# Scan of an RWKV-7 layer: kappa products and query masks moved from a tile's head to its last two levels, prefix sums parted over two levels

## The chip, the core and the metric

The kernel runs on one core of a Trainium2 chip. Time is the device time of one execution in microseconds (us). The engines are TensorE (PE in the profile; its weight loads are PEld), VectorE (DVE), ScalarE (ACT), GpSimd (POOL) and SyncE (SP), which here only issues DMAs. Each runs its own instruction queue in order, and they meet at semaphores.

## What is computed

A two-layer encoder trunk on an input of 256 positions by 1024 channels, all in float32. Both layers have a half-step SwiGLU feed-forward network ahead of and behind their mixer. The mixer of layer 0 is a Hyena convolution beside windowed attention. That of layer 1 is RWKV-7 time mixing in both directions, and the change is in there. Its reference, cut to what matters:

```python
def step(S, inp):
    r_t, w_t, k_t, v_t, a_t, b_t = inp
    sa = jnp.einsum('zbhvk,zbhk->zbhv', S, a_t)
    S = S * w_t[..., None, :] + sa[..., :, None] * b_t[..., None, :] + v_t[..., :, None] * k_t[..., None, :]
    return S, jnp.einsum('zbhvk,zbhk->zbhv', S, r_t)

xs = (shared(r), time_major(decay), time_major(k_dir), shared(v), shared(-kk), time_major(b_dir))
_, ys = lax.scan(step, jnp.zeros((2, B, H, N, N), f32), xs)
y = ys[0] + ys[1][:, ::-1]            # then a norm per head, a bonus, a gate and w_o
```

There are 16 heads of 64 channels, and z is the direction, forward or backward.

## The kernel before

The scan is not run position by position. It is cut into chunks of 64 positions (CH), four to a direction (NCH), and into 8 tiles t of 128 channels (CT), which are two heads each. `tiles` runs t = 0 to 7, unrolled, and every engine has a body for a tile: `pe_tile`, `act_tile`, `dve_tile`, `pool_tile`. A unit u is one chunk of one direction. With p = t % 2, operands lie in two sets of buffers. `AR[p]` holds alpha and the query for a unit, `BB[p]` beta, `KD[p]` kappa (the key).

A tile has a head and five levels:

- **Head.** PE multiplies beta by alpha and the query (into `DBANK`, PSUM banks 1 and 3, L1514), alpha by beta (`ZBANK`, banks 0 and 2, and `CBANK`, banks 4 and 6, L1523 and L1524), and kappa by alpha and the query (`BQBANK`, banks 5 and 7, L1536). A factor or a product in this text is one of these matrices of 64x64 per unit. ACT copies a factor (L1659), and POOL multiplies it by the masks of the five levels (`XL`, L1893). DVE masks the starts of the two inverses (L1790, L1793, L1797), then the part of the beta product that belongs to keys (`AQ`, L1801, called the key mask here), and the kappa product (`BQ`, L1805, called the query mask).
- **Levels n = 0 to 4.** A level doubles the size of the blocks of the triangular inverses, for each direction z: PE multiplies (`zee`), ACT copies the result (L1675), PE multiplies again (`update`), and DVE adds (L1818; L1820 in the last level). PE and DVE do this for z = 0 and then z = 1.
- **Chunk work.** While the levels 0 to 3 of tile t run, chunk n of tile t - 1 is carried through the recurrence: PE `pe_r`, DVE copy (`dve_rc`, L1761), PE `pe_u`, DVE copy (`dve_uc`, L1765), PE `pe_s` and `pe_y`, ACT scales the state (`act_s`, L1652). Tile 0 has no such work beside it.
- **Other work, put by hand between the levels.** PE transposes (`pe_tr`, copied by ACT at L1645) in levels 0 to 2, and after the levels forms the mean (`pe_mean`, L2156) and the gate (`pe_gate`, three matmuls twice). DVE prepares tile t + 1: prefix sums of the log decays (`dve_prefix`, L1709 to L1718) after level 0, beta and kappa (`dve_kb`, L1727 and L1728) after level 1, alpha and the query (`dve_alpha`, L1750 and L1755) after level 3, just ahead of `dve_bonus` (L1742). `dve_rb` (L1735) and `dve_center` (L2276) stand behind level 4. ACT takes the exponentials of the prefix sums (`act_operands`), and POOL multiplies them in (L1877, L1883).

The order on each engine is the order of the code. No scheduler moves anything. `pe_gate` waits for `dve_bonus`, and the head of the next tile follows it on PE. The transposes of level 0 wait for both query masks (`a_ready`), since bank 7 holds the kappa product of z = 1 until then:

```python
pe.wait_ge(a_ready, 2 * t + 2)
pe.wait_ge(vc_ready, t + 1)
```

The weights come in steps of 1.5 MB into the two halves of `raw`. The scan uses one half of it for its own buffers (among them `KD` and `BB` of the odd tiles), so SP loads step S_O + 1 into that half (L2364) only when the last tile no longer needs it. ACT splits what came (L2262) at the end of the scan.

Of the kernel before, what the change touches and what calls it, by code (L numbers as in the profile page):

```python
# [15 lines left out]
P = 128  # L16
C = 1024
L = 256
CT = C // P
# [5 lines left out]
CH = 64  # L25
# [70 lines left out]
def build(nc, io):  # L96
# [7 lines left out]
    with ctx:  # L104
# [1395 lines left out]
        ZBANK, DBANK, BQBANK = (bank[0], bank[2]), (bank[1], bank[3]), (bank[5], bank[7])  # L1500
        CBANK = (bank[4], bank[6])

        def pe_tile(pe, t, p, chunks, ahead):
# [22 lines left out]
            pe.wait_ge(be_ready, 2 * t + 2)  # L1526
            if isinstance(t, int) and t == 0:
                pe.wait_ge(va_read, 2)
            else:
                pe.wait_ge(a_ready, 2 * t)  # L1530
                pe.wait_ge(bo_read, t)
                pe.wait_ge(gt_ready, t) if t > 1 else None
# [26 lines left out]
            for n in range(len(LEVELS)):  # L1559
# [14 lines left out]
                if n in (1, 2):  # L1574
                    pe_tr_wait(pe, t, n)
                for c in range(NCH):
                    last = zee(n, 1, c)
                    if n in (1, 2):
                        tr = pe_tr(pe, p, n, (2 * c, 2 * c + 1))
                last.then_inc(z_done, 1)  # L1580
                if n in (1, 2):
                    tr.then_inc(tr_done, 1)
# [18 lines left out]
                if not ahead and n in (2, 4):  # L1601
                    pe_spread(pe, n // 2 - 1)
            if t:
                pe_mean(pe, t - 1)
# [50 lines left out]
        def act_tile(act, t, p, chunks, ahead):  # L1655
# [8 lines left out]
            for n in range(len(LEVELS)):  # L1664
# [17 lines left out]
                if ahead and n in (1, 2):  # L1682
                    act_operands(act, t + 1, n)
# [18 lines left out]
        def dve_prefix(dve, own, t):  # L1702

            tt, z2 = nc.vector.tensor_tensor, slice(L, 2 * L)
# [3 lines left out]
            for z in range(2):  # L1708
                own(nc.vector.tensor_tensor_scan(out=(CI if z == 0 else CE)[:, z * L:(z + 1) * L], data0=ccols("reset", L),  # L1709
                                                 data1=tile_of(LW, t, z), initial=0.0, op0=ALU.mult, op1=ALU.add))  # L1710
            own.settle()
# [67 lines left out]
        def dve_tile(dve, t, p, chunks, ahead, own):  # L1779
# [5 lines left out]

            for z in range(2):
# [3 lines left out]
                own(tt(TQ[:, z, 1], units_of(DBANK[z])[:, :, 0:CH], mask64("first_incl", z * P), ALU.mult))  # L1790
            for z in range(2):
# [8 lines left out]
            for z in range(2):  # L1800
# [816 lines left out]
```

## Time and profile before

| what | value |
| --- | --- |
| median of 3 runs | 1346.65 us (1345.31 to 1348.06) |
| profiled execution, device time | 1351.68 us |
| its span in the profile | 1349.8 us |
| granted TensorE clock over the span | 0.973 |
| the scan's 8 tiles in it | 855.35 to 1109 us |
| a tile of the scan | 30.3 to 32.0 us, the last some 38 us |

The page of the profile gives the busy time of each engine, and the chain of work that ended last: followed back from the last instruction, at each step to what released it, or to the instruction before it on its engine. Such a chain is the path that sets the time. Idle time of an engine off this path costs nothing. The timeline lists instructions by start, with the idle time ahead of them and who ended it in square brackets. "issue" there means that the engine waited for nothing that the profile shows.
### The profile page before, as it was taken

What the parts mean: (1) busy time and instruction counts of PE and PEld (TensorE: products, weight loads), DVE (VectorE), ACT (ScalarE), POOL (GpSimd) and SP (SyncE); (2) the same over time, 40 slices, a digit from 0 to 9 for tenths busy, and PEclk for the clock granted to TensorE, in tenths of its full rate; (3) what the DMA queues carried; (4) which work ended last, traced back from release to release, by engine and by line L of the source; (5) the groups of instructions that cost most, each with busy time, mean ns of one, the idle gap of its engine ahead of it and who ended that gap; (6) DMA issues with size and microseconds to landing.
All of it is one profiled execution on the core that took longest, in us unless ns stands there. A gap on an engine that the chain in (4) does not pass through costs nothing.

```text
span 1349.8 us, 33102 instructions
## 1 busy us (share of the span) xinstructions
PE 1259.2 (93%) x14080; PEld 1131.4 (84%) x14080; DVE 919.8 (68%) x1270; ACT 644.7 (48%) x1045; POOL 442.0 (33%) x220
## 2 busy tenths in 40 slices
PE   8999999999899999899997899888888889899998
PEld 5899999878799999799996898877777777799998
DVE  7666667786877776766667985656555546866654
ACT  5544446452644455644445368233333333555553
POOL 1344442211244443344443000543334303344442
PEclk9999999999999999999998899789999989999999
DMA  8355555323355555455555342010000012555553
GB/s 332 141 185 184 186 185 173 123 86 140 141 186 186 186 186 200 174 186 186 186 186 187 101 181 95 3 50 4 4 4 4 3 50 95 195 188 186 186 184 119
DMA packets 18676, 188.34 MB, mean 140 GB/s; under 512 B 2064, under 2 KB 2576, under 8 KB 3600
## 3 DMA queue, kind: packets, MB, share of 16 engines
q1 hardware_dynamic: 18576, 186.84, 38.5%
q8 instruction: 83, 1.36, 0.4%
q14 instruction: 17, 0.14, 0.0%
HBM read 185.78 MB, written 1.05 MB: 138 GB/s over the span
## 4 chain that ended last, share of the span: by engine, by line
PE 75%; DVE 15%; ACT 5%; issue 3%; POOL 1%; DMA 0%; SPq 0%; DVEq 0%; ACTq 0%
PE gu_bank L257 22%; PE gu_bank L259 11%; PE bank L236 7%; PE bank L238 7%; PE bank L237 7%; PE bank L1380 5%; PE gu_bank L1411 4%; PE gu_bank L236 3%; PE gu_bank L237 2%; PE gu_bank L238 2%; DVE WL L193 2%; ACT WH L186 1%; DVE XSQ L407 1%; POOL raw L1893 1%; PE gu_bank L1380 1%
## 5 line engine op out<-in xcount | busy, mean ns | idle before, releaser
L202 POOL TENSOR_TENSOR WL<-raw,WH 128x1024 fp32r<-128x1024 f32 x102 | 342.0, 3354 | 597.1 <-ACT WH L187 575.3
L257 PE MATMUL gu_bank<-HX,WH 128*128 128x512 f32 x1408 | 508.2, 403 | 13.8 <-DVE WL L193 12.1
L259 PE MATMUL gu_bank<-HX,WL 128*128 128x256 f32 x1408 | 398.5, 283 | 0.0
L193 DVE TENSOR_TENSOR WL<-raw,WH 128x2048 fp32r<-128x2048 f32 (+1 forms) x114 | 252.6, 2215 | 137.8 <-ACT WH L186 137.7
L257 PEld LDWEIGHTS gu_bank<-HX,WH 128*128 128x128 f32 x1408 | 267.9, 190 | 78.5 <-DVE WL L193 8.5
L259 PEld LDWEIGHTS gu_bank<-HX,WL 128*128 128x128 f32 x1408 | 269.6, 191 | 0.2
L186 ACT ACTIVATE WH<-raw 128x2048 fp32r<-128x2048 f32 (+1 forms) x114 | 204.6, 1795 | 23.4 <-PE gu_bank L238 13.5
L236 PE MATMUL bank<-PH,WH 128*128 128x256 f32 (+1 forms) x720 | 202.0, 284 | 1.0 <-ACT arena L1942 1.0
L237 PE MATMUL bank<-PL,WH 128*128 128x256 f32 (+1 forms) x720 | 201.9, 283 | 0.0
L238 PE MATMUL bank<-PH,WL 128*128 128x256 f32 (+1 forms) x720 | 201.8, 283 | 0.0
L438 ACT ACTIVATE work<-work 128x256 f32<-128x256 f32 x88 | 36.8, 418 | 278.0 <-DVE work L490 278.0
L490 DVE TENSOR_TENSOR work<-work,rstd 128x512 f32<-128x512 f32 x88 | 160.5, 1824 | 3.0
L236 PEld LDWEIGHTS bank<-PH,WH 128*128 128x128 f32 (+1 forms) x720 | 135.5, 190 | 5.3 <-ACT arena L1942 1.4
L238 PEld LDWEIGHTS bank<-PH,WL 128*128 128x128 f32 (+1 forms) x720 | 135.7, 190 | 0.0
L237 PEld LDWEIGHTS bank<-PL,WH 128*128 128x128 f32 (+1 forms) x720 | 135.6, 190 | 0.0
L187 ACT ACTIVATE WH<-raw 128x1024 fp32r<-128x1024 f32 x114 | 118.9, 1043 | 0.0
L236 PE MATMUL gu_bank<-HX,WH 128*128 128x256 f32 x336 | 98.8, 294 | 4.3 <-DVE WL L193 3.0
L237 PE MATMUL gu_bank<-HX,WH 128*128 128x256 f32 x336 | 95.6, 285 | 0.0
L238 PE MATMUL gu_bank<-HX,WL 128*128 128x256 f32 x336 | 95.4, 284 | 0.0
L484 DVE TENSOR_TENSOR work<-gu_bank,work 128x512 f32<-128x512 f32 x88 | 60.4, 686 | 20.7 <-ACT work L434 20.4
L236 PEld LDWEIGHTS gu_bank<-HX,WH 128*128 128x128 f32 x336 | 64.9, 193 | 8.1 <-issue 6.5
L495 DVE TENSOR_TENSOR PL<-work,PH 128x256 fp32r<-128x256 f32 x88 | 37.5, 426 | 48.2 <-ACT PH L441 48.2
(311 smaller groups left out, 2028.2 us busy)
## 6 DMA issues: line engine op xcount, KB each, us to landing
raw<-stream_in SPq DMA_DIRECT2D x114, 1536.0 KB, 6.5
cst<-const_in SPq DMA_DIRECT2D x1, 1568.0 KB, 16.9
X<-xT_in SPq DMA_DIRECT2D x1, 1024.0 KB, 5.6
raw<-stream_in SPq DMA_DIRECT2D x1, 1024.0 KB, 7.6
arena<-hconst_in SPq DMA_DIRECT2D x2, 512.0 KB, 10.8
out<-X SPq DMA_DIRECT2D x4, 256.0 KB, 2.4
arena<-hconst_in SPq DMA_DIRECT2D x1, 768.0 KB, 13.9
arena<-fw_in SPq DMA_DIRECT2D x1, 512.0 KB, 8.4
```

What stands on the lines that cost most here:

```text
L186: nc.scalar.activation(WH[:, slot, :cut], raw[:, slot, :cut], ACT.Copy).then_inc(hi_ready, 1)
L187: nc.scalar.activation(WH[:, slot, cut:end], raw[:, slot, cut:end], ACT.Copy).then_inc(hi_last, 1)
L193: nc.vector.tensor_tensor(WL[:, slot, :cut], raw[:, slot, :cut], WH[:, slot, :cut].bitcast(fp32), ALU.subtract).then_inc(lo_ready, 1)
L202: (eng or nc.gpsimd).tensor_tensor(WL[:, slot, cut:end], raw[:, slot, cut:end], WH[:, slot, cut:end].bitcast(fp32), ALU.subtract).then_inc ...
L236: nc.tensor.matmul(out_ap, wh, xh, start=start, stop=False, **kw)
L237: nc.tensor.matmul(out_ap, wh, xl, start=False, stop=False, **kw)
L238: return nc.tensor.matmul(out_ap, wl, xh, start=False, stop=stop, **kw)
L257: nc.tensor.matmul(out[:, :], WH[:, slot, w:w + P], HX[:, x, :, :].rearrange("p i t -> p (i t)"), start=k == 0, stop=False)
L259: return nc.tensor.matmul(out[:, L:2 * L], WL[:, slot, w:w + P], HH[:, x, :], start=False, stop=k == CT - 1)
L484: nc.vector.tensor_tensor(gus[o], gu_bank[:, o, :, 0:L], gus[o], ALU.add).then_inc(gsum_ready, 1)
L490: nc.vector.tensor_tensor(gus[o], gus[o], both, ALU.mult).then_inc(gs_ready, 1)
L1380: last = nc.tensor.matmul(dst[r, cols], w[r], x[r], start=start, stop=stop)
```

## The change

- The kappa products leave the head. Those of z = 0 are done in level 3 and those of z = 1 in level 4, in turn with the matmuls of `zee(n, 1, c)`, and both into bank 5. `BQBANK` goes.
- The query mask of z = 0 stands on DVE behind the additions of level 3, that of z = 1 behind those of level 4. The kappa product of z = 1 waits for the query mask of z = 0, as they share the bank.
- The key mask of z = 0 stands between the first two masks of the head, that of z = 1 where both were.
- The transposes of level 0 wait for other semaphores, not for the query masks.
- The prefix sums are parted: the two scans inside chunks stay behind level 0, the rest goes behind level 1, and `dve_kb` from level 1 to 2. On ACT `act_operands` goes from levels 1 and 2 to 2 and 3.
- `pe_mean` goes into level 4, ahead of its updates, and `dve_center` ahead of `dve_rb`.
- SP's load of step S_O + 1 waits for the last kappa product as well.

The core of the diff:

```diff
             if n:
                 pe.wait_ge(tr_ready, 3 * t + n)
+                pe.wait_ge(be_ready, 2 * t + 2)
             else:
-                pe.wait_ge(a_ready, 2 * t + 2)
                 pe.wait_ge(vc_ready, t + 1)
+                pe.wait_ge(va_read, 2)
+                pe.wait_ge(bo_read, t)
+                pe.wait_ge(gt_ready, t) if t > 1 else None
...
-            for z in range(2):
-                for c in range(NCH):
-                    u = z * NCH + c
-                    last = heads(BQBANK[z], at64(c, P), kappa[:, u], both(p, u))
-                last.then_inc(bq_done, 1)
+            def kappa_wait(z):
+                pe.wait_ge(be_ready, 2 * t + 2)
+                pe.wait_ge(a_ready, 2 * t + z)
+                if z == 0 and not ahead:
+                    pe.wait_ge(gn_n, 1)
+
+            def kappa_product(z, c):
+                u = z * NCH + c
+                return heads(bank[5], at64(c, P), kappa[:, u], both(p, u))
...
+                elif n > 2:
+                    kappa_wait(n - 3)
                 for c in range(NCH):
                     last = zee(n, 1, c)
                     if n in (1, 2):
-                        tr = pe_tr(pe, p, n, (2 * c, 2 * c + 1))
+                        other = pe_tr(pe, p, n, (2 * c, 2 * c + 1))
+                    elif n > 2:
+                        other = kappa_product(n - 3, c)
                 last.then_inc(z_done, 1)
...
+                if t and n == 4:
+                    pe_mean(pe, t - 1)
...
                 if not ahead and n in (2, 4):
+                    if n == 4:
+                        pe.wait_ge(a_ready, 2 * CT)
                     pe_spread(pe, n // 2 - 1)
...
-                if ahead and n in (1, 2):
-                    act_operands(act, t + 1, n)
+                if ahead and n in (2, 3):
+                    act_operands(act, t + 1, n - 1)
...
                 own(tt(TQ[:, z, 1], units_of(DBANK[z])[:, :, 0:CH], mask64("first_incl", z * P), ALU.mult))
+                if z == 0:
+                    key_mask(0)
...
+            key_mask(1)
...
+                if n > 2:
+                    query_mask(n - 3)
                 if ahead and n == 0:
-                    dve_prefix(dve, own, t + 1)
+                    dve_sums_in_chunk(dve, own, t + 1)
+                if ahead and n == 1:
+                    dve_sums_past_chunk(dve, own, t + 1)
...
-                if ahead and n == 1:
+                if ahead and n == 2:
                     dve_kb(dve, own, t + 1, q)
...
+                if t and n == 4:
+                    dve_center(dve, t - 1)
                 if ahead and n == 4:
                     dve_rb(dve, t + 1)
...
                     sp.wait_ge(z_done, 10 * CT - 4)
+                    sp.wait_ge(bq_done, 2 * CT)
                     load(S_O + 1, 1)
```

What the engines' queues hold, place by place. **DVE, tile 3, from the end of the head to the first copy of level 1**, before (L1761 is `dve_rc`, L1801 the key masks, L1805 the query masks, L1709 to L1718 the prefix sums):

```order
L1761 COPY work<-bank 128x128
L1801 TENSOR_TENSOR work<-gu_bank,cst 128x256 x2
L1805 TENSOR_TENSOR scan_51<-bank,cst 128x512 x2
L1765 COPY work<-bank 128x128
L1818 TENSOR_TENSOR scan<-scan,gu_bank 128x2x64x2 x2
L1709 SCALAR_TENSOR_TENSOR arena<-cst,arena 128x256
L1709 SCALAR_TENSOR_TENSOR scan_51<-cst,arena 128x256
L1712 TENSOR_TENSOR scan_51<-arena 128x256
L1714 COPY small<-scan_51 128x4
L1716 TENSOR_TENSOR scan_51<-small,scan_51 128x256
L1718 TENSOR_TENSOR arena<-scan_51,arena 128x256
L1761 COPY work<-bank 128x128
```

The same place now (L1779 is `dve_rc`, L1805 the key mask, L1723 the scans inside chunks):

```order
L1779 COPY work<-bank 128x128
L1805 TENSOR_TENSOR work<-gu_bank,cst 128x256
L1783 COPY work<-bank 128x128
L1841 TENSOR_TENSOR scan<-scan,gu_bank 128x2x64x2 x2
L1723 SCALAR_TENSOR_TENSOR arena<-cst,arena 128x256
L1723 SCALAR_TENSOR_TENSOR scan_51<-cst,arena 128x256
L1779 COPY work<-bank 128x128
```

One key mask and both query masks have gone from ahead of `dve_uc`, and four of the six instructions of the prefix sums from ahead of the next `dve_rc`.

**DVE, tile 3, from the additions of level 3 to the next tile**, before (L1771 copies the output of tile t - 1, L1750 and L1755 are `dve_alpha`, L1742 `dve_bonus`):

```order
L1818 TENSOR_TENSOR scan<-scan,gu_bank 128x2x8x16 x2
L1771 TENSOR_SCALAR arena<-bank 128x256
L1750 SCALAR_TENSOR_TENSOR scan_51<-arena,scan_51 128x4x64 x2
L1755 TENSOR_TENSOR scan_51<-arena,XSQ 128x4x64 x2
L1742 SCALAR_TENSOR_TENSOR arena<-bank,arena 128x256
L1820 TENSOR_TENSOR arena<-scan,gu_bank 128x4x32 x2
L1735 SCALAR_TENSOR_TENSOR XSQ<-arena,par,XSQ 128x256
L2276 SCALAR_TENSOR_TENSOR arena<-bank,arena 128x256
```

Now (L1810 is a query mask):

```order
L1841 TENSOR_TENSOR scan<-scan,gu_bank 128x2x8x16 x2
L1810 TENSOR_TENSOR scan_51<-bank,cst 128x512
L1789 TENSOR_SCALAR arena<-bank 128x256
L1768 SCALAR_TENSOR_TENSOR scan_51<-arena,scan_51 128x4x64 x2
L1773 TENSOR_TENSOR scan_51<-arena,XSQ 128x4x64 x2
L1760 SCALAR_TENSOR_TENSOR arena<-bank,arena 128x256
L1843 TENSOR_TENSOR arena<-scan,gu_bank 128x4x32 x2
L1810 TENSOR_TENSOR scan_51<-bank,cst 128x512
L2303 SCALAR_TENSOR_TENSOR arena<-bank,arena 128x256
L1753 SCALAR_TENSOR_TENSOR XSQ<-arena,par,XSQ 128x256
```

One query mask now stands ahead of everything that leads to `dve_bonus`, the other behind the last additions.

**PE, tile 3, from the bonus matmul of level 3 to the gate**, before (L1419 is the bonus, L1411 `zee` and `update`, L2156 the mean):

```order
L1419 MATMUL bank<-XSQ,cst 128x256
L1411 MATMUL gu_bank<-scan 64x32 x48
L2156 MATMUL bank<-arena,cst 128x256
L236 MATMUL bank<-GH,WH 128x256
```

Now (the matmuls 64x128 at L1380 are the kappa product of z = 1, L2183 is the mean):

```order
L1419 MATMUL bank<-XSQ,cst 128x256
L1411 MATMUL gu_bank<-scan 64x32 x26
L1380 MATMUL bank<-scan_51,raw 64x128 x2
L1411 MATMUL gu_bank<-scan 64x32 x2
L1380 MATMUL bank<-scan_51,raw 64x128 x2
L1411 MATMUL gu_bank<-scan 64x32 x2
L1380 MATMUL bank<-scan_51,raw 64x128 x2
L1411 MATMUL gu_bank<-scan 64x32 x2
L1380 MATMUL bank<-scan_51,raw 64x128 x2
L2183 MATMUL bank<-arena,cst 128x256
L1411 MATMUL gu_bank<-scan 64x32 x16
L236 MATMUL bank<-GH,WH 128x256
```

Eight kappa matmuls now stand in turn with the eight of `zee(4, 1)`, and the mean ahead of the last updates.

## Rows read from the trace of the kernel before

**Rows 1.** The page, chain of work that ended last: shares by engine.

```profile
PE 75%; DVE 15%; ACT 5%; issue 3%; POOL 1%; DMA 0%; SPq 0%; DVEq 0%; ACTq 0%
```

**Rows 2.** Windows, tile 3: stretch, length, busy by engine, clock, DMA share, GB/s.

```profile
946.45:976.81 30.36, 25.00 (x910) 22.78 (x908) 18.24 (x46) 10.93 (x35) 11.14 (x13) 1.00 0.02 4
```

**Rows 3.** Chain of tile 3, head to level 1: start, us, what.

```profile
948.28 2.42 POOL raw L1893 x2
...
952.41 1.28 DVE scan L1805 x2
...
955.75 0.97 DVE arena L1709
```

**Rows 4.** Timeline of PE, tiles 3 and 0: start, us, instruction, idle ahead.

```profile
953.74 0.68 PE L1380 MATMUL bank<-cst,XSQ 64*64 64x64 f32 x16 [0.77 <-DVE scan L1805]
...
959.02 0.39 PE L1380 MATMUL bank<-work,arena 64*64 64x64 f32 x6 [1.08 <-DVE work L1761]
...
968.46 0.30 PE L1411 MATMUL gu_bank<-scan 64*64 64x32 f32 x4 [0.71 <-issue]
...
867.38 0.39 PE L1411 MATMUL gu_bank<-scan,raw 64*64 64x32 f32 x3 [2.73 <-DVE scan L1818]
```

**Rows 5.** Timeline of DVE, tiles 1, 3 and 4: level 0, then levels 2 to 4.

```profile
893.54 0.42 DVE L1818 TENSOR_TENSOR scan<-scan,gu_bank 128x256 f32<-128x256 f32 x1 [2.57 <-PE gu_bank L1411]
...
955.41 0.42 DVE L1818 TENSOR_TENSOR scan<-scan,gu_bank 128x256 f32<-128x256 f32 x1 [1.20 <-PE gu_bank L1411]
...
966.59 0.42 DVE L1818 TENSOR_TENSOR scan<-scan,gu_bank 128x256 f32<-128x256 f32 x1 [0.74 <-PE gu_bank L1411]
967.75 0.29 DVE L1761 COPY work<-bank 128x128 f32<-128x128 f32 x1 [0.74 <-PE bank L1380]
...
971.61 0.42 DVE L1818 TENSOR_TENSOR scan<-scan,gu_bank 128x256 f32<-128x256 f32 x1 [1.68 <-PE gu_bank L1411]
...
972.28 1.43 DVE L1750 SCALAR_TENSOR_TENSOR scan<-arena,scan 128x256 f32<-128x256 f32 x2
...
974.31 0.41 DVE L1742 SCALAR_TENSOR_TENSOR arena<-bank,arena 128x256 f32<-128x256 f32 x1
...
1004.22 1.01 DVE L1750 SCALAR_TENSOR_TENSOR scan<-arena,scan 128x256 f32<-128x256 f32 x2
```

**Rows 6.** Groups of PE in tile 3: the 16 kappa matmuls, busy us, mean ns.

```profile
L1380 PE MATMUL bank<-scan,raw 64*64 64x128 f32 x32 | 1.9, 270 | 0.0
```

**Rows 7.** Chain of tile 4, end of its level 4.

```profile
1004.12 1.68 PE gu_bank L1411 x48
1005.79 0.63 PE bank L2156 x2
```

**Rows 8.** Chain of tile 0 and into tile 1.

```profile
862.39 1.11 DVE arena L1709
...
881.65 3.52 POOL WL L202
```

**Rows 9.** Windows round places where PE idles; columns as in rows 2.

```profile
864.60:867.40 2.80, 0.07 (x4) 0.05 (x2) 2.72 (x6) 0.56 (x2) 1.35 (x2) 0.91 0.02 6
867.40:878.30 10.90, 10.90 (x266) 10.18 (x268) 4.59 (x12) 3.52 (x12) 3.27 (x3) 0.50 0.01 3
...
950.27:953.74 3.47, 1.81 (x64) 1.48 (x64) 2.20 (x6) 0.57 (x2) 3.47 (x6) 1.00 0.00 0
...
888.60:892.00 3.40, 2.60 (x76) 2.41 (x78) 2.36 (x6) 0.38 (x1) 3.40 (x6) 0.82 0.60 251
```

**Rows 10.** End of the scan: SP's loads, ACT behind them, us to landing.

```profile
1090.53 39.59 SPq L2354 DMA_DIRECT2D raw<-stream_in  x3
...
1109.28 1.04 ACT L2262 ACTIVATE WH<-raw 128x1024 fp32r<-128x1024 f32 x1
1111.68 0.52 ACT L1652 ACTIVATE arena<-bank,small 128x64 f32<-128x64 f32 x2 [1.35 <-PE bank L1380]
...
raw<-stream_in SPq DMA_DIRECT2D x3, 1536.0 KB, 6.7
```

More of the change, by code:

```diff
@@ L1497, in pe_y @@
             last.then_inc(y_done, 1)
-        ZBANK, DBANK, BQBANK = (bank[0], bank[2]), (bank[1], bank[3]), (bank[5], bank[7])
+        ZBANK, DBANK = (bank[0], bank[2]), (bank[1], bank[3])
         CBANK = (bank[4], bank[6])
@@ L1525, in pe_tile @@
                 last.then_inc(a_done, 1)
[L1526 to L1532, printed above, removed]
-            for z in range(2):
-                for c in range(NCH):
-                    u = z * NCH + c
-                    last = heads(BQBANK[z], at64(c, P), kappa[:, u], both(p, u))
-                last.then_inc(bq_done, 1)
+            def kappa_wait(z):
[6 more added lines that the diff above has]
+                return heads(bank[5], at64(c, P), kappa[:, u], both(p, u))
             def zee(n, z, c):
@@ L1578, in pe_tile @@
                     if n in (1, 2):
-                        tr = pe_tr(pe, p, n, (2 * c, 2 * c + 1))
+                        other = pe_tr(pe, p, n, (2 * c, 2 * c + 1))
+                    elif n > 2:
+                        other = kappa_product(n - 3, c)
                 last.then_inc(z_done, 1)
                 if n in (1, 2):
-                    tr.then_inc(tr_done, 1)
+                    other.then_inc(tr_done, 1)
+                elif n > 2:
+                    other.then_inc(bq_done, 1)
+                if t and n == 4:
+                    pe_mean(pe, t - 1)
                 if step and n == 0:
@@ L1702, in dve_prefix, with dve_sums_in_chunk @@
         def dve_prefix(dve, own, t):
-            tt, z2 = nc.vector.tensor_tensor, slice(L, 2 * L)
+            dve_sums_in_chunk(dve, own, t)
+            dve_sums_past_chunk(dve, own, t)
+        def dve_sums_in_chunk(dve, own, t):
             if not (isinstance(t, int) and t == 0):
@@ L1710, in dve_prefix, with dve_sums_past_chunk @@
                                                  data1=tile_of(LW, t, z), initial=0.0, op0=ALU.mult, op1=ALU.add))
+        def dve_sums_past_chunk(dve, own, t):
+            tt, z2 = nc.vector.tensor_tensor, slice(L, 2 * L)
             own.settle()
@@ L1784, in units_of, with key_mask, query_mask @@
                 return b[:, :].rearrange("p (c s) -> p c s", c=NCH)
+            def key_mask(z):
+                tt(AQ[p][:, z * NCH:(z + 1) * NCH, :], units_of(DBANK[z])[:, :, CH:P], mask64("first_incl", z * P + CH),
+                   ALU.mult).then_inc(aq_read, 1)
+            def query_mask(z):
+                dve.wait_ge(bq_done, 2 * t + z + 1)
+                tt(BQ[p][:, z * NCH:(z + 1) * NCH, :], units_of(bank[5]), mask("strict_incl", z), ALU.mult).then_inc(a_ready, 1)
             for z in range(2):
@@ L1799, in dve_tile @@
                 dve_rc(dve, t - 1, 0)
-            for z in range(2):
-                tt(AQ[p][:, z * NCH:(z + 1) * NCH, :], units_of(DBANK[z])[:, :, CH:P], mask64("first_incl", z * P + CH),
-                   ALU.mult).then_inc(aq_read, 1)
-            for z in range(2):
-                dve.wait_ge(bq_done, 2 * t + z + 1)
-                tt(BQ[p][:, z * NCH:(z + 1) * NCH, :], units_of(BQBANK[z]), mask("strict_incl", z), ALU.mult).then_inc(a_ready, 1)
+            key_mask(1)
             for n in range(len(LEVELS)):
@@ L1840, in dve_tile @@
                 dve_low(dve, 0)
-            if t:
-                dve_center(dve, t - 1)
         def pool_mix0(pool):
```

1 line of the change is left out of this document (removed).

## Prediction

> **What bounds the kernel now.** I began with the page's chain that ended last: PE holds 75% of it and DVE 15%, DMA nothing [rows 1]. All that the change touches lies in the scan, so I cut the trace into its tiles. Tile 3 takes 30.36 us with PE busy for 25.0 and DVE for 18.2 [rows 2]. Neither is full. Inside a tile the path changes hands, and each edit must be read from the wait that it stands in. The chain of tile 3 shows three places. In the head POOL's first two mask products (2.42 us) hold all others. Then come the query masks (1.28), then, behind level 0, the prefix sums [rows 3]. The timeline of PE says what that costs it: 0.77 us idle for the query masks and 1.08 for the copy that stands behind the prefix sums [rows 4]. These two are what the change can win in a tile. The rest of PE's idle time there is "issue", or POOL.
>
> **Kappa products out of the head: nothing won.** The 16 matmuls are busy for 1.9 us, some 1.6 from first to last start, so 0.8 for each z [rows 6]. But they ran while the path went through ACT and POOL, and POOL does not start sooner without them. PE then idles in the head where it worked.
>
> **Query masks out of the head: -0.77 a tile.** The transposes of level 0 no longer wait for them. DVE has 1.28 less ahead of `dve_uc` and the first addition [rows 3], so nothing on that side is late next. I take the whole idle time. Tiles 1 to 6: -4.6. The key mask between the first two masks has DVE idle time to stand in.
>
> **Prefix sums parted: -1.0 a tile.** PE was free at 959.02 - 1.08 = 957.94, so with the 0.77 above at 957.17. The two scans now start at 955.75 - 0.77 = 954.98. At the length of the first in tile 3 (0.97) both take at most 1.94, with the copy of 0.3 they end at 957.2, which costs nothing over PE's own end. At the length they had in tile 0 (1.11 each [rows 8]) it is 957.5, and 0.75 remains of the 1.08. I take 1.0, nearer the tile that is costed: -6.0 in six tiles. The other four instructions stand behind level 1 in the place of `dve_kb`, of about the same length, and `dve_kb` goes to level 2. There the last addition starts at 966.59 and the next `dve_rc` at 967.75 [rows 5], and four instructions of at most 0.42 need 1.4 to 1.7. So `dve_rc` comes at 968.3 to 968.6, 0.55 to 0.9 late.
>
> **Kappa products in level 3: +0.55 a tile.** PE has 0.8 us more ahead of `pe_u` of chunk 3. It waited for that same `dve_rc` (967.75 and 0.29, so 968.1 without the issue gap of 0.71 that the trace has there [rows 4]). Extra matmuls and the later copy lie beside one another, and the later of them counts. Without any cover it is +0.8, with a lucky issue gap 0.3. Six tiles: +3.3.
>
> **Query mask and kappa product in level 4: +0.3 to +0.6.** This is the step against the change. From the start of the last addition of level 3 (971.61) to the start of the bonus operation (974.31) DVE needs 2.70, and the gate, and behind it the next head, wait for that [rows 5]. A query mask of 0.6 (half of 1.28) now stands in it. Some comes back. The first pair of `dve_alpha` took 1.43 in tile 3 and 1.01 in tile 4 [rows 5], the longer where it ran beside POOL, and it now runs later. That gives 3.4 to the gate against 3.16 (974.77 less 971.61) before. On PE the same stretch took 2.87 in tile 4, of which 1.68 and 0.63 are the last `zee`, the updates and the mean [rows 7]. There the mask adds 0.5 and the kappa product 0.8, and the mean, moved into the wait for ACT's copy, gives 0.6 back: 3.5. I take +0.3 in four tiles and +0.6 in two, +2.4. The bounds are 0 and +1.4 a tile. The second query mask and `dve_center` find DVE idle ahead of the next head.
>
> **Tile 0: -4.5.** It has no chunk work. PE idles there for 2.73 us until the whole prefix sums are through [rows 4], and the clock fell in that stretch (0.91), then stood at 0.50 for the 10.9 us of levels 2 to 4, with PE busy all the time [rows 9]. With only two scans ahead of the additions (2.2 us [rows 8]) 2.3 us of this idle time go. If the clock then stays at 2.4 GHz, half of the 10.9 goes as well, against 1.6 of kappa products and 0.6 of query mask. That would be -5.5. I keep 1.0 back, since levels also hold copies that the clock does not shorten. ACT's split and POOL's part of it (3.52 [rows 8]), which hold up tile 1, start behind the last levels and move along.
>
> **Tile 7 and the load: +0.8.** -0.77 as before, no prefix sums. At its end `pe_spread` and so the gate wait for the second query mask too: two masks (1.2) and 0.8 of kappa, less 0.7 for the mean, is +1.3, so +0.5. The load of S_O + 1 was issued at 1090.53 and needs 6.7 us to land. Now it is issued with the last kappa product, at about 1104, and lands at 1111. ACT wanted it at 1109.28, but had 1.35 us idle behind its split [rows 10]. Of a delay of 1.2 nearly all fits in there. I take +0.3, at most +1.5.
>
> **The clock in the heads: +2.8.** Without the kappa products PE idles some 2.7 of 3.8 us in each head. A stretch of 3.47 us with 1.81 busy kept the clock at 1.00 in tile 3, one with 2.60 busy had 0.82 in tile 1 [rows 9]. Such a fall cost tile 1 1.4 us: DVE waited 2.57 for the second addition of level 0 against 1.20 [rows 5]. I count it in two more heads. The Trainium skill, page "TensorE: Matmul & The Clock Gate", section "Part 1: The HAM clock gate", says that the throttled state is the default and that activity releases it. By that rule thinner heads are a cost of this change that the diff does not show. Tile 0's fall within an idle stretch agrees.
>
> **Sum.** -4.6 - 6.0 + 3.3 + 2.4 - 4.5 + 0.8 + 2.8 = -5.8. The profiled execution took 1351.68 us (span 1349.8, 1.9 around it), which gives 1345.9. It lies 0.4% above the median of the runs. On the median the sum gives 1346.65 - 5.8 = 1340.8.
>
> **Rivals.**
>
> - *The clock falls in tile 0 all the same.* For it: tile 0 has light matmuls only, and its clock did not come back for 10.9 us. Against it: it fell only when PE stood still. Then the kappa products cost double, 3.2, and tile 0 is +1.0 instead of -4.5: 1346.3.
> - *The prefix scans are held by POOL.* They start 0.8 sooner, into POOL's mask products, and both might take the 1.11 of tile 0 and a POOL operation ahead of them, or PE's issue gaps of 0.7 eat what is won. Half of the 1.0 a tile goes, +3.0: 1343.8. The Trainium skill, page "SBUF — State Buffer", section "Who interferes with whom", says that a DVE instruction with two inputs in SBUF contends with a GpSimd instruction that reads SBUF, and that the port pair is locked for a whole instruction. By this rule the scans wait out whole POOL operations. The lengths 0.97 and 1.11 of the same scan agree that something of the kind happens.
> - *Slower: the heads lose the clock.* In every tile PE now idles over 2 us in a row but for one short burst, the clock falls in the six heads (8.4 instead of 2.8) and, by the same mechanism, in tile 0 (+5.5). That is -5.8 + 5.6 + 5.5 = +5.3: 1352.0. Against it stands the full clock of tile 3 [rows 2], with idle time of half that length in its head. It decides from four extra falls beside tile 0's.
> - That the change does not do what it says is out: the queues hold the new order.
>
> **How the numbers follow.** The forecast has 0.58 (1334 to 1344.5 by its own bounds), tile 0's clock 0.12, the scans 0.15, the slower case 0.15. A measurement of this kernel tells about 0.2%, 2.7 us, from no change. Faster than 1343.9: 0.55 of the forecast, 0.09 of the scans, 0.02 of tile 0, so 0.66. Slower than 1349.3: 0.15 and 0.02. The rest is 0.17. The range 1334 to 1348 leaves out the slower case and a little at the low end.
>
> **What would show it.** In the changed kernel's trace: no idle time of PE for query masks ahead of the transposes of level 0; under 0.4 us of it ahead of `pe_u` in level 1; a middle tile of 29.4 to 30.0 us; `dve_rc` of chunk 3 at the end of `dve_kb`; 3.4 us from the last addition of level 3 to the gate; the clock at 1.00 in tile 0's levels 2 to 4, and tile 1's first mask 4 to 5 us sooner; ACT's first split of S_O + 1 ended by a DMA. The forecast is wrong if the clock is below 1.00 in most tiles, if the stretch to the gate grows by more than 1 us, or if tile 0 keeps its 30 us.

## The result, and the profile after

The changed kernel is slower. Its median is 1354.3 us (1349.1 to 1359.5 in 17 runs) against 1348.9 us for the kernel before on the same chip; the ratio is 1.0033, with a 95% interval of 1.0017 to 1.0049, so about 4.5 us more. The forecast was 5.8 us less, and the range ended at 1348. The profiled execution took 1359.5 us, its span is 1357.5.

The windows show where to look. Columns are as in rows 2; these are tile 0, tile 1, and tile 3 of the changed kernel, then 10 us near the end of its tile 1.

```profile
856.74:881.02 24.28, 19.49 (x736) 18.11 (x732) 17.70 (x37) 11.85 (x29) 13.11 (x14) 0.93 0.02 4
881.02:919.79 38.77, 30.46 (x836) 27.67 (x838) 18.12 (x47) 10.67 (x33) 13.29 (x14) 0.78 0.13 44
...
950.85:981.38 30.53, 26.04 (x910) 23.72 (x908) 17.82 (x47) 10.94 (x35) 11.14 (x13) 0.94 0.02 4
...
909.02:919.02 10.00, 9.23 (x100) 7.88 (x99) 4.89 (x13) 1.95 (x7) 1.30 (x2) 0.51 0.01 2
```

Tile 0 is 3.2 us shorter than before (27.52), tile 1 is 5.3 longer (33.45), with half the clock at its end. Tile 3 took 30.53 against 30.36 [rows 2]. The next view takes 9 us of tile 3, from 3 us behind its first mask: the kernel before, then the changed one.

```profile
949.45:958.45 9.00, 6.33 (x250) 5.61 (x246) 6.27 (x15) 2.62 (x9) 6.72 (x10) 1.00 0.02 4
```

```profile
953.85:962.85 9.00, 7.94 (x282) 7.57 (x284) 4.38 (x10) 2.75 (x9) 6.72 (x10) 0.81 0.02 5
```

The clock is 0.81 where it was 1.00. The same window has 0.81 in tiles 0, 3, 4, 5, 6 and 7, 0.62 in tile 1, and 1.00 in tile 2 alone. The timeline of PE in the head of tile 3 tells what happens ahead of it (start, us, instruction, idle ahead):

```profile
954.01 0.66 PE L1411 MATMUL gu_bank<-scan,raw 64*64 64x32 f32 x16 [1.41 <-POOL raw L1920]
955.14 0.48 PE L1411 MATMUL gu_bank<-scan,raw 64*64 64x32 f32 x10 [0.47 <-POOL raw L1920]
956.28 0.39 PE L1380 MATMUL bank<-work,arena 64*64 64x64 f32 x6 [0.43 <-DVE work L1779]
```

The 0.77 for the query masks [rows 4] is gone, as forecast, and so is the 1.08 ahead of the copy. In its place stands 1.41 us of idle time for POOL, where PE had worked on the kappa products. Last, the chain of work at the end of the same tile, level 3 to the gate:

```profile
975.78 0.69 DVE scan L1810
...
977.29 0.44 PE bank L1380 x8
977.73 0.63 PE bank L2183 x2
978.36 1.05 PE gu_bank L1411 x32
979.41 0.32 PE bank L236
```

The first query mask (L1810), the second kappa products, the mean (L2183), the updates and the gate follow each other with hardly a gap. From the last addition of level 3 to the gate it is 3.88 us, in five of its seven tiles; before it was 2.73 to 3.16 in the middle tiles.

For all kernels below I cut the middle tiles (2 to 6) at the starts of DVE's additions and took the mean of each piece. "start>L0" runs from the tile's first mask to the first addition of level 0, "L0" from there to the second addition of that level, ">L1" from that one to the first addition of level 1, and so on; the gate is its first matmul, and the next tile begins with its first mask. All in us, from one profiled execution each:

```
kernel               start>L0  L0  >L1   L1  >L2   L2  >L3   L3  >gate >next   sum
before                 7.35  1.61 4.57 1.32 3.56 1.37 3.46 2.63 2.99  2.04  30.90
changed                6.53  2.25 3.21 1.41 4.03 1.62 3.99 2.23 3.88  2.04  31.19
changed, again (h3)    6.90  2.50 2.92 1.40 4.25 1.71 3.83 2.28 3.89  2.04  31.71
sums parted (e1)       7.35  1.61 3.29 1.74 4.38 1.50 3.57 2.35 3.07  2.04  30.90
heads filled (e3)      6.40  1.40 3.69 2.01 4.07 1.75 3.79 2.34 3.88  2.04  31.38
one early (g2)         6.63  2.27 3.02 1.42 3.98 1.69 3.89 2.23 3.13  2.04  30.29
```

In the changed kernel the head gains, the second addition of level 0 is later (the clock), and the way to level 1 gains 1.4 or more. The rest of the tile gives it all back. The two looks at the same kernel differ by 0.5 us a tile, so a difference of that size between two rows shows nothing.

### The profile page after: what moved, and what is told of

The parts are those of the page before. It is cut to its first block, busy times and chain, and to the rows that moved or that the text cites. A ratio compares the mean times of both kernels' runs of the same rounds, so it can differ in the third digit from the quotient of the medians.

```text
span 1357.5 us, 33127 instructions
## 1 busy us (share of the span) xinstructions
PE 1260.6 (93%) x14080; PEld 1130.2 (83%) x14080; DVE 918.5 (68%) x1270; ACT 643.9 (47%) x1045; POOL 441.6 (33%) x220
## 3 DMA queue, kind: packets, MB, share of 16 engines
q8 instruction: 83, 1.36, 0.4%
## 4 chain that ended last, share of the span: by engine, by line
PE 76%; DVE 13%; ACT 5%; issue 3%; POOL 2%; DMA 0%; SPq 0%; DVEq 0%; ACTq 0%
PE gu_bank L257 21%; PE gu_bank L259 11%; PE bank L236 7%; PE bank L238 6%; PE bank L237 6%; PE bank L1380 6%; PE gu_bank L1411 5%; PE gu_bank L236 3%; PE gu_bank L238 3%; PE gu_bank L237 3%; DVE WL L193 2%; ACT WH L186 2%; POOL raw L1920 1%; DVE XSQ L407 1%; PE gu_bank L1380 1%
## 5 line engine op out<-in xcount | busy, mean ns | idle before, releaser
L186 ACT ACTIVATE WH<-raw 128x2048 fp32r<-128x2048 f32 (+1 forms) x114 | 204.6, 1795 | 22.7 <-PE gu_bank L238 13.5
L236 PE MATMUL gu_bank<-HX,WH 128*128 128x256 f32 x336 | 100.5, 299 | 4.6 <-DVE WL L193 3.0
L237 PE MATMUL gu_bank<-HX,WH 128*128 128x256 f32 x336 | 97.3, 289 | 0.0
L1685 ACT ACTIVATE scan<-gu_bank 128x128 f32<-128x128 f32 x80 | 22.3, 279 | 101.5 <-PE gu_bank L1411 101.5
```

The lines of the kernel that those rows point to most:

```text
L186: nc.scalar.activation(WH[:, slot, :cut], raw[:, slot, :cut], ACT.Copy).then_inc(hi_ready, 1)
L236: nc.tensor.matmul(out_ap, wh, xh, start=start, stop=False, **kw)
L237: nc.tensor.matmul(out_ap, wh, xl, start=False, stop=False, **kw)
```

## Experiments

Ratios are to the kernel before, from runs on the same chip. Two changes recur. "Parted" is the change's edit of the prefix sums alone:

```
-                if ahead and n == 0: dve_prefix(dve, own, t + 1)
-                if ahead and n == 1: dve_kb(dve, own, t + 1, q)
-                if ahead and n in (1, 2): act_operands(act, t + 1, n)
+                if ahead and n == 0: dve_sums_in_chunk(dve, own, t + 1)
+                if ahead and n == 1: dve_sums_past_chunk(dve, own, t + 1)
+                if ahead and n == 2: dve_kb(dve, own, t + 1, q)
+                if ahead and n in (2, 3): act_operands(act, t + 1, n - 1)
```

"Shifted" puts waits that are long fulfilled into PE's program, ahead of tile 0:

```
+            for _ in range(64):
+                pe.wait_ge(kk_rec, 1)
             pe.wait_ge(kk_ready, 1)
```

**Each half alone.** e1 is the kernel before with the parted sums.

> The kernel before with the prefix sums parted and nothing else: the scans behind level 0, the other four instructions behind level 1, the factors' products behind level 2, ACT's operands a level later. Kappa products and query masks stay in the head. Theory A (the heads have lost the clock): the heads stay full, so the clock holds, and only the gain is left: 1.0 us in each of six tiles, and about 2 us of the idle time of tile 0, so 6 to 8 us less than before, 1341 to 1343. Theory B (the last two levels are what costs): the same here, 1341 to 1343. Theory C (parting the sums wins nothing, since dve_rc of chunk 3 comes late or POOL holds the scans): within 1 us of before, 1348.

Measured: 0.9989 (0.9967 to 1.001), 1.5 us less, and not clear of nothing, where 6 to 8 were expected by theories A and B. e2 is the changed kernel with that edit undone.

> The changed kernel with its prefix sums whole again: only the kappa products, the query masks, the key mask, the mean and dve_center are moved. Theory A (clock) and theory B (last levels) both have all of the loss in this half: the measured +4.5 us and the 6 to 8 us that the parted sums had given, so 10 to 12 us more than before, 1359 to 1361. Theory C (the sums win nothing): as the changed kernel, 4 to 5 us above before, 1353. A and B differ in where: A has the granted clock under 0.9 in the first 9 us of most tiles, B has 0.8 us or more in each tile between the last addition of level 3 and the gate.

Measured: 1.0047 (1.0023 to 1.007), +6.4 us where theories A and B expected 10 to 12. Their signs are both there: the clock is 0.62 to 0.81 early in all five middle tiles, and the stretch to the gate is 3.88 us. The halves add up, -1.5 + 6.4 = +4.9 against the measured +4.5, though each is only known to about 3 us. So the move of the masks loses, and the parted sums, of which some 10 us were hoped for (6.0 and tile 0's 4.5), hardly win.

Where e1's gain went is in its row of the table: 4.57 to 3.29 on the way to level 1, a gain of 1.28, and then +0.42, +0.82, +0.13, +0.11, -0.28 and +0.08, which is +1.28. The waits of PE over the scan (us in total, times, longest) show the exchange. Before:

```profile
PE bank L1380 <- DVE work L1761: 12.1, 15, 1.8
PE bank L1380 <- issue: 7.9, 10, 1.4
PE gu_bank L1411 <- issue: 6.6, 12, 1.4
```

and e1:

```profile
PE gu_bank L1411 <- issue: 11.3, 14, 1.4
PE bank L1380 <- issue: 10.1, 14, 1.2
PE bank L1380 <- DVE work L1769: 5.8, 13, 0.6
```

6.3 us of waiting for DVE's copy went, and 6.9 us of "issue" came. To see what "issue" is, I numbered PE's weight loads, matmuls and waits in the order of the records. In the kernel before (15 of them), the changed one (18), e1 (24), e4 (29) and g2 (22), every idle stretch of PE over 0.3 us in the scan that is put down to "issue" ends at an instruction whose number is 129 above a multiple of 256, or at the matmul right behind that weight load. I call these places edges. The page's table of queues (queue, packets, MB, share) has transfers of instructions of 1.36 MB / 83 = 16.4 KB:

```profile
q8 instruction: 83, 1.36, 0.4%
```

In the scan 55 of them stand beside 55 edges of PE. In e1 three in a row ended at 959.39, 963.46 and 967.46, and PE went on from its next edges at 960.83, 964.88 and 968.84, each 1.4 us later. I read this so: in these three PE used up its 256 instructions before the next ones were there. The Trainium skill, page "Advanced Engine Details and Errata", section "Sequencer and Instruction Queues" (ISA Cache), gives 16 KB, 256 instructions, as the cache line of an engine's program; the trace agrees with both numbers.

**The edges.** g1 is the kernel before, shifted with 128 waits.

> The kernel before with 128 waits that are long fulfilled put into PE's program ahead of tile 0, where PE waits for DVE, and nothing else changed: every later instruction of PE stands 128 places further back. In the trace of before 17 idle stretches of PE over 0.3 us (14.7 us in all with the shorter ones) end at an instruction whose number among PE's weight loads, matmuls and waits is 129 above a multiple of 256, and the queue records of that trace show one transfer of 16 KB for every 256 of PE's instructions. Theory D (PE stands still at the edges of these blocks until the next block of its program is there): the stretches move to other work, 128 instructions away in program order, all again at one and the same remainder, and their sum stays between 10 and 20 us; the time moves by up to 3 us either way. Rival E (they belong to the work where they stand, a matmul or a wait that is slow there): they stay at the same matmuls of level 2 and level 3, at another remainder, and the time is that of before within 1 us.

> The kernel with the sums parted and one query mask late (e4), with 64 fulfilled waits put ahead of tile 0 in PE's program. Theory D (stops at the edges of PE's blocks of 256 instructions): the 27 us of idle time at the edges in e4 stay at one remainder, now 64 instructions away in the work, and their sum changes by a few us with the place at which the edges fall; the time is that of e4 within 4 us either way. Rival E: the stretches stay with their matmuls and the time with e4's within 1 us.

Measured: 0.9968 (0.9948 to 0.9989), e4's time within the noise, so here the time says nothing and the places of the stops decide. PE's timeline in tile 4, e4 first (1132nd and 1388th instruction):

```profile
990.21 0.60 PE L1411 MATMUL gu_bank<-scan 64*64 64x32 f32 x27 [1.11 <-issue]
...
994.25 0.24 PE L1411 MATMUL gu_bank<-scan 64*64 64x32 f32 x1 [1.33 <-issue]
```

and g3 (1100th and 1356th), where one stop has moved to other matmuls, the transposes:

```profile
989.07 0.38 PE L1382 MATMUL bank<-cst,scan 64*64 64x64 f32 x5 [0.95 <-issue]
...
992.85 0.24 PE L1413 MATMUL gu_bank<-scan 64*64 64x32 f32 x1 [0.70 <-issue]
```

PE's idle time in us from the first mask of tile 0 to that of tile 7 (the pieces over 0.1 us), at the edges and elsewhere, and how long the clock stood at 1.2 GHz there:

```
kernel          at edges  elsewhere  us at half clock
before             11.3      22.5        24
changed            15.6      23.4        34
e1                 19.2      15.3        17
e2                  9.1      32.6        34
e3                 20.7      14.0        10
e4                 23.9       9.7        10
g2                 16.5      13.5        20
h4 (g2 shifted)    22.7      12.6        10
```

The kernels that wait less elsewhere mostly wait more at the edges: from before to e1 7.2 us less and 7.9 more, from e1 to e4 5.6 less and 4.7 more. Theory D holds. The exchange is not complete in every kernel: g2, among the fastest, has the smallest sum, 30.0.

**The clock.** e3 is the changed kernel with the head filled:

```
+            for z in range(2):
+                for c in range(NCH):
+                    kappa_product(z, c)
+
             def zee(n, z, c):
```

> The changed kernel with the 16 kappa products issued in the head as well, into the bank where the late ones are written again; nobody reads the early ones. They only give PE work in the head. Theory A (clock): the granted clock in the first 9 us of the middle tiles goes from 0.81 back to 1.00, each of five or six tiles is 1.0 to 1.4 us shorter, and the time is 6 to 7 us below the changed kernel, 1346 to 1348. Theory B (last levels): the extra products bring nothing, the time stays at the changed kernel's 1353 to 1354, or is 1 to 2 us longer where they delay a product of level 0.

Measured: 0.997 (0.9948 to 0.9991), 8.5 us below the changed kernel, and its 9 us in tile 3:

```profile
950.06:959.06 9.00, 7.50 (x332) 7.05 (x332) 5.06 (x11) 2.74 (x9) 7.50 (x10) 1.00 0.02 4
```

Products that nobody reads give the clock back in tile 0 and in all middle tiles, and the time falls, as theory A has it. But the profiled middle tiles do not show the gain that it forecast there: 31.38 us against 31.19 and 31.71 in the two looks at the changed kernel. The way to level 1 is shorter, and 20.7 us stand at the edges where 15.6 stood. Also, 64 more instructions a tile (32 weight loads and 32 matmuls) move the edges. i1 and i2 repeat the pair with both kernels shifted.

> The changed kernel with 64 fulfilled waits put ahead of tile 0 in PE's program, so that the edges of PE's blocks of 256 instructions fall on other work. It is the one half of a pair with the filled heads at the same edges. By the traces so far the changed kernel stands at half clock in the head of nearly every tile, its stretch from the last addition of level 3 to the gate is 3.88 us, and nothing of both depends on the edges: the same here, 1.002 to 1.005 of before.

> The same with the 16 kappa products issued in the head as well (the filled heads, 64 waits further back). Without the shift the filled heads were timed at 0.997 of before against 1.0033 for the changed kernel, 8.5 us, while the stages of the profiled middle tiles show 0.7 us a tile between them and the first two tiles up to 5. If the price of the lost clock in the heads is what the stages show (theory A at 0.5 to 1 us a tile, and the long stretch in tile 1 by chance on top), this one is 3 to 7 us below its other half. If the 8.5 us were the luck of where the edges fell, the two are equal within 2 us here.

Measured: i1 1.0012 (0.9994 to 1.0031), i2 0.9982 (0.9961 to 1.0002). The gap is 4.0 us, in the range of theory A. i1 itself came out below its 1.002 to 1.005: with 32 instructions put far ahead, the changed kernel is not measurably slower than before, so part of its 4.5 us may hang on where its edges fall. And again the middle tiles of i2 are not shorter (a sum of 31.72 against 31.34). That filling wins is shown twice; where in the kernel it wins is not. The same 9 us of tile 6, i1 and then i2:

```profile
1042.29:1051.29 9.00, 7.94 (x282) 7.57 (x284) 4.14 (x10) 2.74 (x9) 6.72 (x10) 0.81 0.02 4
```

```profile
1042.30:1051.30 9.00, 6.87 (x292) 6.40 (x290) 4.76 (x10) 2.75 (x9) 7.51 (x10) 1.00 0.01 4
```

i1 kept 1.00 in tiles 3 and 4, with the changed kernel's thin head, and needed 11.23 and 11.42 us to level 1 there, against 12.05 in its tiles 5 and 6 at 0.81. And g1 lost it in tiles 2, 4 and 6 with the full head of before, at the same idle pieces of 0.5, 0.4 and 0.8 us. A thin head makes the fall likely, it does not force it.

h1 thins the heads of the kernel before and moves nothing. It leaves out 12 of the 16 kappa products in each tile from 1 on, so it does not compute the layer:

```
-                for c in range(NCH):
+                for c in range(1 if t else NCH):
                     u = z * NCH + c
                     last = heads(BQBANK[z], at64(c, P), kappa[:, u], both(p, u))
```

> The kernel before with three of four kappa products of each z left out in the heads of tiles 1 to 7 (12 matmul pairs of 16; the masks then read what stands in the bank), all else where it was. It takes work away and moves nothing. Theory A (a thin head loses the clock): the granted clock in the first 9 us of most middle tiles is 0.81 instead of 1.00, and the kernel is 3 to 8 us slower than before although it does less, 1352 to 1357. Theory B (the last levels are what costs): nothing of it is touched here, so equal to before or up to 1 us faster, and the heads keep the clock. Theory D allows 2 us either way, since 24 instructions less in each tile move the edges of PE's blocks.

Measured: 1.0001 (0.9981 to 1.0022). Its tile 3:

```profile
954.97:963.97 9.00, 6.84 (x230) 6.40 (x232) 5.16 (x12) 2.28 (x8) 7.04 (x10) 0.81 0.01 4
```

All five middle tiles have 0.62 to 0.81 there. The clock went as theory A said, and the cost did not come: 3 to 8 us were expected, and none is measured, within 3 us. In the profile the way to level 1 is 0.9 us a tile longer (14.42 against 13.54). So work was removed, the clock went with it, and no time was won or lost. h2 issues the kappa products of before twice.

> The kernel before with its 16 kappa products issued twice in each head, the second time over the first. Theory A (clock): the middle tiles of before had 1.00 in their first 9 us already, so they win nothing, and only tile 0 and tile 1, where before stood at half clock for 17 and 8 us, can win: 0 to 4 us less than before, 1345 to 1349. By theory D part of that comes back: 32 more instructions a tile are an eighth of a block more. Theory B: equal, or 1 us longer for the second products.

Measured: 1.001 (0.9993 to 1.0027): no gain where 0 to 4 us were expected, the products now stand in the head's path (8.2 us to the first addition instead of 7.35). They are 64 more instructions a tile in the records, weight loads included, not the 32 of the expectation. More filling is not better.

h3 is the changed kernel, profiled again.

> The changed kernel once more, for a second profile. Its two stretches at half clock in tile 1, the second one 10 us long at the end of the tile, are either what the kernel does in each execution, or come and go. If they come and go, tile 1 takes 33 to 34 us here instead of 38.8, the middle tiles have 0.81 in their first 9 us again, and the stretch from the last addition of level 3 to the gate is again 3.88 us, as in the first profile.

Measured: tile 1 took 34.82 us, tile 0 23.60, both without the long fall, and the middle tiles lost the clock in all five heads. This tile 1:

```profile
879.32:914.14 34.82, 26.37 (x836) 24.01 (x838) 18.12 (x48) 10.37 (x33) 13.31 (x14) 0.90 0.14 49
```

So the fall at the end of tile 1 comes and goes. e1's profile has it too (tile 0, tile 1, and its 10 us):

```profile
855.17:878.18 23.01, 18.95 (x716) 17.59 (x715) 18.86 (x37) 11.19 (x27) 13.19 (x14) 1.00 0.02 4
878.18:915.09 36.91, 31.47 (x871) 29.14 (x863) 18.48 (x48) 11.38 (x34) 13.31 (x14) 0.77 0.13 46
904.18:914.18 10.00, 10.00 (x123) 8.81 (x120) 4.00 (x11) 1.43 (x5) 1.99 (x2) 0.50 0.01 4
```

**The last levels.** e4 has the parted sums, the kappa products in the head, and of the masks the one of bank 7 there too; the one of bank 5 stands behind the last addition.

```
+            query_mask(1)
+            if not ahead:
+                query_mask(0)
...
                 if ahead and n == 4:
+                    query_mask(0)
                     dve_rb(dve, t + 1)
```

> The kernel before with the sums parted as in e1, and of the two query masks the one of bank 7 taken first in the head, the one of bank 5 at the end of level 4 behind the last addition. Kappa products stay in the head, nothing is added in front of the gate. Theory A (clock) and theory B (last levels) both expect what e1 gives and 0.5 to 0.6 us a tile more for the mask that is gone ahead of the transposes: 3 to 4 us less than e1, 1337 to 1340. If the 0.77 us of idle time ahead of the transposes was never on the path, it is equal to e1 within 1 us.

Measured: 0.9962 (0.994 to 0.9983), -5.1 us. That is 3.6 less than e1, the 3 to 4 expected of the one mask; what is missing of the forecast 1337 to 1340 is what e1 missed. g2 keeps the change's single bank, with the products of z=0 in the head and those of z=1 in level 3:

```
+            for c in range(NCH):
+                last = kappa_product(0, c)
+            last.then_inc(bq_done, 1)
...
             key_mask(1)
+            query_mask(0)
...
-                if n > 2:
-                    query_mask(n - 3)
+                if n == 4:
+                    query_mask(1)
```

> The changed kernel with the kappa products of z=0 (8 matmul pairs of 16) back in the head, in the same bank, their query mask in the head behind the second key mask, the products of z=1 in level 3 and their mask behind the last addition of level 4. No query mask and no kappa product stands ahead of the gate's operands any more. Theory A (the clock falls because the heads are thin): half the work is back, so the clock is 1.00 in at least some of the middle tiles' first 9 us; with all of them at 1.00 the time is 7 us below the changed kernel for the clock and 3 to 4 for the last levels, 1343 to 1346; with the clock still at 0.81 there it is 1349 to 1351. Theory B (the last levels are what costs) expects 3 to 5 us less than the changed kernel, 1349 to 1351, whatever the clock does. Theory D expects part of each gain back as idle time at the edges of PE's blocks, over 20 us in all there against 17.8 in the changed kernel.

Measured: 0.9954 (0.9937 to 0.9972), 6.2 us faster than before and 10.6 faster than the changed kernel. Its stretch to the gate is back at 3.13, and its clock still at 0.81 in tiles 3 to 6. Seven stretches shorter by 0.75 are 5.3 us, what theory B gave it at most. The other 5 us are more than the noise of about 3, and no run says where they come from. g4 adds the products of z=1 to that head as a filling, h4 is g2 shifted.

> As the run with the products of z=0 in the head, and ahead of them the 8 products of z=1 as well, into the same bank, which the ones of z=0 overwrite: the head holds as many kappa products as before. Theory A (clock): 1.00 in the first 9 us of all middle tiles, so where that run has lost the clock in a head this one is 1.2 us shorter for each, 1343 to 1346 in all; where that run has kept it, the two are equal within 1 us. Theory B: no gain from the extra products, equal or 1 us longer.

> The kernel with the products of z=0 in the head and those of z=1 in level 3 (the fastest so far), with 64 fulfilled waits put ahead of tile 0 in PE's program. Theory D: the idle stretches at the edges of PE's blocks stand 64 instructions away in the work, their sum is between 14 and 24 us, and the time is within 4 us of that kernel's, 1341 to 1349; if the shift helps as it did with the other kernel (27 us at the edges down to 21), it is the fastest of all, 1341 to 1343.

Measured: g4 0.9952 (0.9925 to 0.9978), h4 0.9955 (0.9938 to 0.9973). Both have 1.00 in that 9 us window of all middle tiles, and neither is measurably faster than g2. Tile 3, g2 and then h4:

```profile
944.20:953.20 9.00, 7.93 (x282) 7.58 (x284) 4.62 (x11) 2.77 (x9) 6.73 (x10) 0.81 0.02 4
```

```profile
945.66:954.66 9.00, 7.25 (x314) 6.80 (x315) 5.47 (x12) 2.75 (x9) 7.50 (x10) 1.00 0.01 4
```

h4 waits 22.7 us at the edges and g2 16.5. With the gate's path short, a head at half clock costs nothing that can be measured here, though 3 us in all would not be seen. That PE at full clock only arrives at the next edge too early fits these numbers, but is not shown.

## Why the prediction was wrong

**Query masks out of the head, -0.77: right at its place, and too small.** With the clock kept (e3) the head is 6.40 against 7.35 and the next addition 1.40 against 1.61: -1.16 a tile. The one mask that e4 takes out is the only part of it that timed runs show by itself, 3.6 us, known to about 3.

**Prefix sums parted, -1.0: the step that failed most.** The wait went, with 1.28 us in the middle tiles of e1, more than forecast (it had been 1.37 on their mean; tile 3, from which the term was sized, has one of the smaller ones). What failed is that the won time was taken to be kept. The step asked only which engine is late next, and no engine was: PE's own program was. Of the 10.5 us of this term and tile 0's, e1 measured 1.5. The "issue" gap of 0.71 [rows 4] was taken as a matter of luck that might cover other things. It is a stop at the edge of a block, with another of 0.96 us ahead of it in that tile; such stops grow by what is saved ahead of them. The five middle tiles of e1 have the mean of before in the profile, 30.90 and 30.90.

**Tile 0, -4.5: near in the tile, wrong for the sum.** e1's tile 0 was 4.51 us shorter at a clock of 1.00, the changed kernel's 3.2 and 3.9. Tile 1 gave some or all of it back. Tiles 0 and 1 together took 60.97 us before, 59.92 in e1, and 63.05 and 58.42 in the two looks at the changed kernel. The difference between those two is mostly the fall at the end of tile 1, which I had not thought of: with it the stretch to the gate is 6.08 us instead of 3.88, and from there to the next tile 4.80 instead of 2.75. Why the clock falls there is open. Stops at block edges stand ahead of it, of 0.96 and 1.10 us in the changed kernel's tile 1 and of 0.71 and 0.67 in e1's, but the second look at the changed kernel has the same 0.96 and 1.10 and no fall.

**Kappa products in level 3, +0.55: about right.** The way from level 2 to level 3 is 3.79 to 3.99 against 3.46.

**Last levels, +0.3 to +0.6: mis-sized.** It is 3.88 against a mean of 2.99, +0.89 a tile, 5.3 in six tiles where 2.4 stood. The price of the mask and of the products was right. What failed was "the mean, moved into the wait for ACT's copy, gives 0.6 back". The chain shows products, mean and updates end to end on PE, with no wait in which the mean could hide, and the 0.6 is paid in full.

**Tile 7 and the load, +0.8: open.** From its first mask to the end of the span it was 279.0 us before, 281.8 and 277.9 in the two looks, too wide a spread. The load was issued at 1107.78 and 1105.31, later than the 1104 of the forecast. It landed at 1114.12 and 1111.48, and ACT's first split started 0.14 and 0.07 us later. Only in the second look was ACT idle ahead of it, for 0.55 us. So the load cost 0.55 us at most in these two looks, and the +0.5 of the gate there is not separated.

**The clock in the heads, +2.8: the fall right in kind, the count too low, the price not settled.** I counted two more heads and got six or more. The price was put at 1.4 us for each. In the table the changed kernel needs 11.99 and 12.32 us from the first mask to level 1, e3 11.49: 0.5 to 0.8 a tile. The timed pairs with filling say 8.5 and 4.0 us in all, each to about 3; h1, which loses the clock in every middle tile, and g2 beside h4 show no cost at all. One number for a fall does not exist here. That it depends on what PE would wait for next is my reading, and the spread stays open.

**The rivals.** The slower case named 1352.0, and its falls of the clock came. Their cost is shown in part only, and that its time came so near is luck in good part: its +5.5 for tile 0 did not come (by the prediction's own 2.3, 3.2 and 0.6 it should have been +6.0), and block edges and last levels stand in its place. The rival of the prefix scans named POOL and, in half a sentence, PE's issue gaps that eat what is won. POOL did not hold them: in the changed kernel the two scans together took 1.35 to 1.91 us in the middle tiles, a mean of 1.65 against 1.63 before, and the way to level 1 gained in full. The gaps did it, and took not half but nearly all.

The middle tiles of the changed kernel, in its two looks: -1.54 and -1.21 to level 1 with the fall in it, +0.81 and +1.11 through level 2, +0.53 and +0.37 on the way to level 3, -0.40 and -0.35 in level 3, +0.89 and +0.90 to the gate. That is +0.3 and +0.8 a tile, where the forecast's terms had -0.8 without its two falls.

## What to carry to other kernels

Before a wait is removed, ask of idle time that the profile calls "issue" whether it stands at a fixed distance in instructions. If it does, the engine's program is itself a resource, and a microsecond saved just ahead of such an edge can come back there. Moving work out of a stretch where the engine is idle anyway wins nothing, and may cost the clock behind it (it cost time in two pairs here, and none in two others); work moved onto the path of the last stage is paid in full unless a wait that stays is named for it. Here the way to win was to take out of the gate's path what the change had put in, and keep the rest.

## What was not expected of the hardware

- PE stopped at the 256th of its instructions where it used them up too fast: 9 to 24 us of the scan. It went on 1.2 to 1.6 us after the end of a 16 KB transfer, and blocks ahead of such a stop took mostly 3.4 to 4.1 us.
- 128 fulfilled waits ahead of the scan made it start 4.8 us later and took the room of 64 instructions. 64 of them, in the other shifted kernels, went into PE's idle time there: those scans start at 854.6 to 856.4 us, the unshifted ones at 854.6 to 856.7.
- The granted clock fell to 1.2 GHz behind the same head (idle pieces of 0.5, 0.4 and 0.8 us) in one kernel and not in another that differs by 64 instructions far ahead (0.70 against 1.00 in tile 2).
- In tile 1 the clock stood at 1.2 GHz for 10 us with PE busy for 9.2 and 10.0 of them, in two of the profiles and not in a second one of the same kernel.
